# Input projection, retention, group norms and attention heads: from four programs a layer to two

## The reference, cut to what matters

```python
h = rmsnorm(x, norms[0]) * (1 + sc1) + sh1
aq, ak, av, af, bq, bk, bv, bg, ca, cb = split_cols(jnp.dot(h, w_in))
logf = jax.nn.log_sigmoid((af + b_f).astype(F32))
o_a = attn_fn(aq, ak, av, logf)                       # 4 heads x 128, causal softmax with a bias
q_b, k_b = rope(bq, pos), rope(bk, pos) * (DKB ** -0.5)
r, ret_s = retention(q_b, k_b, bv, ret_s0, ret_chunk) # 4 heads x 64, chunks of 128 tokens
r = _standardize(r).reshape(n, L, WB) * ret_gn_g
o_b = r * jax.nn.silu(bg)
u = ca * jax.nn.sigmoid(cb)
cv, conv_state = causal_dwconv(conv_ctx, u, conv_w, conv_b)   # 31 taps, 256 channels
o_c = jax.nn.silu(layernorm(cv, conv_ln_g, conv_ln_b))
mix = jnp.dot(jnp.concatenate([o_a, o_b, o_c], axis=-1), w_o)
x = x + g1 * rmsnorm(mix, norms[1])
```

## Time and profile before

| what | value |
|---|---|
| median of 3 runs | 3267.7 us (3264.27 to 3270.58) |
| the profiled execution, its own time | 3262.0 us |
| its span, from the first to the last instruction | 3260.2 us |
| PE busy | 2951.3 us (91% of the span) |
| DVE busy | 1751.8 us (54%) |
| ACT busy | 1146.1 us (35%) |
| POOL busy | 336.8 us (10%) |
| mean granted TensorE clock | 0.925 |

### The profile page before, as it was taken

The page is one execution under the profiler, slowest core; times in us unless marked ns, Lnnn a source line. Parts: engine busy times, 40 slices in busy tenths (PEclk is TensorE's granted clock), DMA queues, the critical chain, the costliest instruction groups (busy, mean ns, idle before and its releaser), DMA issues. The chain is left out here.

```text
span 3260.2 us, 45129 instructions
## 1 busy us (share of the span) xinstructions
PE 2951.3 (91%) x17756; PEld 2467.0 (76%) x17756; DVE 1751.8 (54%) x2765; ACT 1146.1 (35%) x1825; POOL 336.8 (10%) x166
## 2 busy tenths in 40 slices
PE   6798789979999999999767997998799999999996
PEld 3586477748878889999726865777388788899996
DVE  1396322243676676676615943223446766766765
ACT  1231123224444354444312311233235444454442
POOL 4111001013200000000042200100231000000000
PEclk7897699989999999999868966999799999999998
DMA  8311011143223332333182100111422333332331
GB/s 329 100 39 24 14 40 32 32 130 97 79 90 97 91 97 90 93 91 91 42 324 55 36 13 21 33 33 45 147 87 84 93 95 91 97 92 85 98 91 68
DMA packets 366283, 276.03 MB, mean 85 GB/s; under 512 B 24125, under 2 KB 308325, under 8 KB 365822
## 3 DMA queue, kind: packets, MB, share of 16 engines
q1 hardware_dynamic: 354896, 267.27, 26.3%
q10 hardware_dynamic: 11214, 6.41, 0.6%
HBM read 259.22 MB, written 15.26 MB: 84 GB/s over the span
## 5 line engine op out<-in xcount | busy, mean ns | idle before, releaser
L1536 PE MATMUL tslot<-g_hi,w_hi 128*128 128x260 f32 (+1 forms) x2496 | 672.9, 324 | 7.6 <-DVE g_lo L2065 6.1
L1536 PE MATMUL tslot<-g_hi,w_lo 128*128 128x260 f32 (+1 forms) x2496 | 667.0, 322 | 0.0
L1536 PE MATMUL tslot<-g_lo,w_hi 128*128 128x260 f32 (+1 forms) x2496 | 664.8, 321 | 0.0
L1536 PEld LDWEIGHTS tslot<-g_hi,w_hi 128*128 128x128 f32 x2496 | 416.4, 190 | 48.9 <-DVE g_lo L2065 6.2
L1536 PEld LDWEIGHTS tslot<-g_hi,w_lo 128*128 128x128 f32 x2496 | 415.4, 189 | 37.9
L1536 PEld LDWEIGHTS tslot<-g_lo,w_hi 128*128 128x128 f32 x2496 | 415.5, 190 | 37.4
L1507 ACT ACTIVATE w_hi<-w_raw 128x1024 fp32r<-128x1024 f32 x292 | 307.1, 1052 | 315.4 <-PE tslot L1854 311.8
L2126 DVE TENSOR_TENSOR cat<-cat,tslot 128x512 f32<-128x512 f32 (+1 forms) x320 | 220.4, 690 | 192.5 <-PE tslot L1854 191.3
L1511 DVE TENSOR_TENSOR w_lo<-w_raw,w_hi 128x1024 fp32r<-128x1024 f32 x256 | 311.8, 1218 | 0.0
L1854 PE MATMUL tslot<-f_hi,w_hi 128*128 128x260 f32 (+1 forms) x1056 | 283.6, 323 | 6.7 <-DVE w_lo L1511 4.5
L1854 PE MATMUL tslot<-f_hi,w_lo 128*128 128x260 f32 (+1 forms) x1056 | 282.0, 322 | 0.0
(11 more groups left out here) (320 smaller groups left out, 4052.8 us busy)
## 6 DMA issues: line engine op xcount, KB each, us to landing
w_raw<-in_ffn_up_dram SPq DMA_DIRECT2D x176, 512.0 KB, 3.7
a_raw<-in_ada_w_dram SPq DMA_DIRECT2D x24, 2048.0 KB, 17.1
w_raw<-in_ffn_down_dram SPq DMA_DIRECT2D x88, 512.0 KB, 3.3
w_raw<-in_w_in_dram SPq DMA_DIRECT2D x46, 512.0 KB, 3.9
w_raw<-in_w_o_dram SPq DMA_DIRECT2D x32, 512.0 KB, 3.7
kp<-in_cache_k_dram SPq DMA_DIRECT2D x32, 256.0 KB, 3.0
xrow<-in_x_prompt_dram SPq DMA_DIRECT2D x8, 512.0 KB, 8.8
out_k_prompt_dram<-k_tok SPq DMA_DIRECT2D x8, 512.0 KB
```

Source lines behind the costliest of these rows:

```text
L1536: last = pe.matmul(out[:, at + a:at + b], w[:, kk, :], x[:, kk, t0 + a:t0 + b], start=(kk == 0 and first), stop=(kk == KD - 1 and w is w_lo))
```

## The change

`block_retention`, `block_group_norms` and `block_heads` become one program, `block_mixer`, and the last two tiles of `block_project` (the gates, i = 10 and 11) move into it. A layer has one barrier where there were three. The mixer makes 14 tiles in 42 passes: each tile in three passes of 344 columns, one pass 24 matmuls. Behind each pass all engines do a fixed piece of other work: retention chunks in phases 1 to 9, group norms in phases 11 to 31, attention in phases 9 to 45, nine phases a head. The gates' tiles are the last two, passes 36 to 41.

Twelve of the 62 taps leave `block_project` and are done by VectorE in phases 1 to 12. The low parts of tiles 1 to 13 are made by VectorE (`low`) in the mixer; that of its first tile is made by GpSimd at the end of `block_project`.

The mixer needs room, so the residual `k.x` is written to a tensor in device memory (`x_hold`) during `block_project`, its place serves the mixer as working space, and it is read back in `block_samples`. The convolution's input `u` moves into `cat` 4 and 5 without its 30 zero columns; a tap now covers only the columns that it reaches.

The diff, cut to its core:

```diff
+TAPS_EARLY = 50
+def conv_tap(k, dve, n):
+    j, w = divmod(n, CONV_W)
+    w = CTX - w
+    u, acc = k.cat[:, 4 + j, :], k.cat[:, 6 + j, CTX - w:TP]
...
+    return dve.scalar_tensor_tensor(acc, u[:, 0:TP - CTX + w], k.vecs[:, 1, 2 * w + j:2 * w + j + 1], acc, ALU.mult, ALU.add)
 def block_project(k, L):
-    tiles = [COL_CA, COL_CA + DC, COL_CA + P, COL_CA + DC + P] + [COL_BQ + P * j for j in range(8)]
+    tiles = [COL_CA, COL_CA + DC, COL_CA + P, COL_CA + DC + P] + [COL_BQ + P * j for j in range(6)]
-        u = sb("u", [P, 2, CTX + NT])
+        u = k.cat[:, 4:6, :]
-            for m, col in enumerate([COL_F] + tiles):
+            for m, col in enumerate([COL_F] + tiles + [2 * HA * DA]):
...
             sp.dma_start(d["conv_sample"][L, :, 0:CTX - 1, :], d["state_conv"][L, :, 1:CTX, :]).then_inc(stored, 16)
+            sp.dma_start(k.x_hold.rearrange("p (a b) -> p a b", b=NT), k.x[:, :, :]).then_inc(stored, 16)
...
-                taps(at, at + 8)
-                at += 8
+                if i < 7:
+                    taps(at, at + 8)
+                    at += 8
...
-            taps(at, len(todo))
+PASS = ((0, 344), (344, 688), (688, NT))
+def block_mixer(k, L):
+        @block.sync
+            def load(n):
+                if n >= 3:
+                    sp.wait_ge(lo_done, n - 2)
+                sp.dma_start(k.w_raw[n % 2][:, :, :], w_in[:, :, column(n):column(n) + P]).then_inc(loaded[n % 2], 16)
...
+        @block.tensor
+            def dense_pass(p):
+                n, (a, b) = p // 3, PASS[p % 3]
+                if p % 3 == 0 and n >= 1:
+                    pe.wait_ge(lo_done, n)
+                if p >= 2:
+                    pe.wait_ge(evac, p - 1)
+                for kk in range(KD):
+                    for w, x, first in ((w_hi, k.h_hi, True), (w_hi, k.h_lo, False), (w_lo, k.h_hi, False)):
+                        last = pe.matmul(dense[p % 2][:, 0:b - a], w[:, kk, :], x[:, kk, a:b], ...)
+                last.then_inc(pass_done, 1)
...
+            for p in range(LAST):
+                if p < N_PASS:
+                    dense_pass(p)
+                h, at = phase(p)
+                if p == 0:
+                    samples()
+                if 2 <= p <= 9:
+                    back(p - 2)
+                if 1 <= p <= 8:
+                    front(p - 1)
+                if p >= 9:
+                    attention(h, at)
+                if 12 <= p < 21:
+                    norm_sums(p - 12)
+                if 11 <= p < 20:
+                    norm_mean(p - 11)
+                if 23 <= p < 32:
+                    norm_rows(p - 23)
+        @block.scalar
...
+                if n >= 3 * HA:
+                    act.activation(k.cat[:, 4 + n - 3 * HA, a:b], out, ACT.Silu).then_inc(evac, 1)
...
+        @block.vector
+            for p in range(LAST):
+                if p == 0:
+                    low(1)
+                    samples_out()
+                if 1 <= p <= 8:
+                    prepare(p - 1)
+                if 1 <= p <= 2 * CONV_W - TAPS_EARLY:
+                    clink(conv_tap(k, dve, TAPS_EARLY + p - 1))
+                if 2 <= p <= 9:
+                    update(p - 2)
...
+                if p % 3 == 2 and (p + 4) // 3 < N_TILES:
+                    low((p + 4) // 3)
 def block_samples(k, L):
             ahead.load(sp)
+            sp.dma_start(k.x[:, :, :], k.x_hold.rearrange("p (a b) -> p a b", b=NT)).then_inc(x_back, 16)
+            sp.wait_ge(x_back, 16)
 def trunk(nc, dram):
-                    run(block_retention, L)
-                    run(block_group_norms, L)
-                run(block_heads, L)
+                    run(block_mixer, L)
```

More of the change, by code:

```diff
@@ L732, in block_retention @@
-        vst = sb("vst", [P, 2 * S, DB])
         small = sb("small", [P, 2, 2 * S])
         pre = sb("pre", [P, NC8 * HA])
[L735 to L742, removed]
+        s0 = prob[0][:, :].rearrange("p (a s e) -> p a s e", a=2, s=S)
@@ L823, in _, with turn_blocks @@
-            pe.wait_ge(state_loaded, 32)
-            for hh in range(2):
-                for s in range(S):
-                    for hp in range(2):
-                        rows = slice(64 * hp, 64 * hp + 64)
-                        last = pe.matmul(o_bank[rows, S * hh + s:S * hh + s + 1], s0[rows, hh, s, :],
-                                         qr[rows, hh, TP + s:TP + s + 1], start=True, stop=True)
-            last.then_inc(samp_ready, 1)
-            for c in range(NC8):
-                if c + 1 < NC8:
-                    front(c + 1)
-                back(c)
+            def turn_blocks(src):
+                for c in range(NC8):
+                    last = pe.transpose(turn[:, P * c:P * c + P], src[:, P * c:P * c + P], ident)
+                last.then_inc(turned, 1)
@@ new lines, in spread_bias, with turn_values @@
+            def spread_bias(h):
+                pe.wait_ge(diag_ready, h + 1)
+                if h == 0:
+                    pe.wait_ge(att_done, NC8)
+                else:
+                    pe.wait_ge(top, NC8 * h)
+                for a, b in HALVES:
+                    last = pe.matmul(sc[:, a:b], ones, bias[:, a:b], start=True, stop=True)
+                last.then_inc(bias_ready, 1)
+            def turn_values(h):
+                if h == 0:
+                    pe.wait_ge(kv_moved, NC8)
+                else:
+                    pe.wait_ge(p_moved, NC8 * h)
+                pe.wait_ge(evac, 9 * h + 3)
+                turn_blocks(vf)
@@ new lines, in turn_keys @@
+            def turn_keys(h):
+                pe.wait_ge(tok_moved, 3 * h + 1)
+                pe.wait_ge(evac, 9 * h + 9)
+                turn_blocks(kf[h % 2])
+                if h == 0:
+                    pe.wait_ge(r_moved, NC8)
+                else:
+                    pe.wait_ge(o_moved, NC8 * h)
+                for n, src in enumerate((kf[h % 2], vf)):
+                    last = pe.matmul(o_bank[0:S, P * n:P * n + P], src[:, TP:NT], ident, start=True, stop=True)
+                last.then_inc(turned, 1)
@@ new lines, in values @@
+            def values(h, i):
+                pe.wait_ge(p_moved, NC8 * h + i + 1)
+                if i < 4:
+                    pe.wait_ge(tok_moved, 3 * h + 3)
+                    if i == 2:
+                        pe.wait_ge(o_moved, NC8 * h + 2)
+                else:
+                    pe.wait_ge(o_moved, NC8 * h + i)
+                at = P * (i % 4)
+                for c in range(i + 1):
+                    row = P * (ROW_AT[i] + c)
+                    last = pe.matmul(o_bank[:, at:at + P], v_tok[h % 2][:, P * c:P * c + P], prob_t[:, row:row + P],
+                                     start=(c == 0), stop=(c == i))
+                last.then_inc(o_ready, 1)
```

893 lines of the change are left out of this document (465 added, 428 removed).

## The result

The changed kernel took 3097.1 us (median of 4 runs, 3092.6 to 3099.0), the kernel before on the same chip 3266.0 (3262.7 to 3270.6). The ratio is 0.948, with a 95% interval of 0.9463 to 0.9496: 169 us less, where 133 less had been forecast. The profiled execution has a span of 3096.3 us against 3260.2.

The account below looks back on a forecast made before the run. TensorE was taken as the bound, losing time to idle waits, three barriers and a low clock. Terms summed to 353.0 us a layer against 419.7, 133.4 less over two layers, giving 3134; own range 3100 to 3160, 8 in 10 reaching 3205.

Parts of the forecast that it names:

- barrier in front, barrier behind: Either side of the merged program: 2.8 us for last read-out and barrier, 1.6 us for the barrier to the samples' program.
- Retention: Retention chunks: 4.2 us each at the full clock, 33.6 us for eight; bounds 3.9 and 7.77 a chunk.
- Rival A: Retention phases: the clock falls again because chunks are too thin to hold it; 3221, or 3178 for half; chance 0.2.
- Heads: Attention with each head's own three tiles: 61.6 us of TensorE busy time a head, 246.4 a layer, idle 7.4 a head gone.
- New passes: At the 42 dense passes: weight loads can't run ahead over a wait, 0.24 us each, 10.1 us a layer.
- Norms: Group norms: means 7.6, spread 9.5 and sums of squares 8.0, together 25.1 us against a stretch of 41.7.
- Projection: Projection without gate tiles: ends with ScalarE's read-out of tile i = 9, begun at 268.46; VectorE ends near 267.1.
- Taps, low parts, table loads, residual: Side work on VectorE, ScalarE and transfers: hidden under passes or other work, so nothing added to the sum.
- B: Attention phases: fixed engine order lets late steps stop those behind, 54 us a layer; 3242, half 3188; chance 0.12.
- C: Last tiles, phases 36 to 41: ScalarE's table loads are on the path, 15.4 us a layer; 3165; chance 0.05.
- D: The residual's write and read-back: its transfers stand out, 12 us a layer; 3158; chance 0.04.
- E: First 32 phases: small pieces keep the clock at 0.50, 253 us more a layer, about 3640, slower; chance 0.04.

Follow-up runs that it names:

- both improvements: Changed kernel with tile 10's high part made before ScalarE's swap copies in the projection, and 16 taps moved to the mixer in place of 12: 3084.7 us, ratio 0.9456.

## Why the prediction came out as it did

The mechanism was right: a full clock in the retention, and passes that cover the waits. The forecast was 37 us too high, nearly all of it in one group of terms: the merged stretch is 17.5 us shorter than forecast in the first layer and 19.1 in the second (353.0 less 335.5 and 333.9). Some smaller things cancel by luck: between the two profiled executions the time fell by 163.8 us, 6.7 less than the two stretches gave (84.2 + 86.3), while the 5.7 us that the forecast added from profiled execution to median were not there in the changed kernel (3098.2 and 3097.1). Per layer, from the end of tile i = 9, with the starts of the phases on TensorE's timeline (a pass's 24 products 3.88 us apart from start to next; phase 0 11.08, phase 1 5.06, phases 2 to 8 8.48 each):

| term | forecast | measured |
|---|---|---|
| barrier in front, barrier behind | 2.8 + 1.6 | 2.65 + 1.6 |
| phases 0 to 8 and `back(7)`: samples' part, 8 chunks, 9 passes, clock at the start | 5.7 + 33.6 + 34.0 + 2.2 + 2.0 = 77.5 | 11.08 + 5.06 + 7 x 8.48 + 3.3 = 78.8 |
| the other 33 passes | 33 x 3.78 = 124.7 | 33 x 3.88 = 128.0 |
| attention, norms, gaps at 33 passes, uncovered end | 110.4 + 25.1 + 7.9 + 3.0 = 146.4 | 335.5 less the rest = 124.5 |
| sum | 353.0 | 335.5 |

**Retention.** Right, with its size a little off: a chunk costs 8.48 - 3.88 = 4.6 us, not 4.2; 0.4 x 8 = 3.2 us a layer. The upper end of the bound, 7.77, was real: cutting the passes gave it back, and a wait. The lower end, 3.9, was not reached: at a clock of 1.00 a pair of products takes 0.72 us where it took 1.22 at 0.50, so not all of a chunk follows the clock. Rival A asked whether a chunk can hold the clock once it is begun. It can, behind a pass; alone it can't.

**The term that was mis-sized** is "attention, norms and the pieces behind the passes", 146.4 us for 124.5. 4.0 of the measured ones are idle time (2.9 + 1.1, forecast 3.0), so the work itself took 120.5. Phases 32 to 40 hold the nine attention pieces of one head and no norms, each behind a pass, and let the rest be divided:

```profile
517.62:576.43 58.81, 58.81 (x382) 53.49 (x381) 20.33 (x56) 33.05 (x49) 0.00 (x0) 1.00 0.06 19
```

Less nine passes of 3.88 this is 23.9 us of attention a head, where the forecast had 27.6 (61.6 less nine passes). The stretch from phase 9 to 31, 174.5 us, less its 23 passes, `back(7)` and the attention in it leaves some 22 us for the norms. So the 21.9 us too many divide, in the order of their size:

- "Heads", 61.6 us busy each: 3.7 us a head too much, 15 in all. Busy time up to a wait holds the modelled end of the last product before it. The head of the earlier trace rows, 480 to 549, had nine waits of TensorE, six of them for ScalarE's copy; in the changed kernel there is none in the middle. The same four instructions, before the change and after it:

```profile
529.78 1.51 PE L1153 MATMUL hslot<-kf,q 128*128 128x512 f32 x4
```

```profile
575.27 1.51 PE L962 MATMUL sc<-x_res 128*128 128x512 f32 x4
```

Before, the wait of 2.19 us is counted from their end, 1.51 us after their start; after, the next pass starts at 576.43, 1.16 after it. Nine times some 0.35 us is most of the 3.7; that all nine are alike is an estimate.
- "New passes", 42 x 0.24 = 10.1, of which 7.9 are in this term. TensorE has no gap at a pass: its idle time in the merged program is 5.66 us, and that at the end. The 0.24 was taken from weight loads that stood behind a wait; with the semaphore long given most of it is gone. What is left stands in the rows of the passes: 3.88 us in place of 3.78, since the second product of a pass starts 0.26 us behind the first and not 0.16. That is 0.1 each, 4.2 us a layer for 10.1.
- "Norms", 25.1, added from the busy times of groups, some 3 too many. Such a sum counts the time in which instructions overlap twice. The changed kernel shows it: its groups for norms add up to 24.8 us, as forecast, for some 22 of time, and those for attention to 119.8, for four times 23.9. The forecast knew that ends are modelled and gave 4 us a layer for it in the heads, as a lower end.

Against these stand some 4 us at the end that had no term: 1.0 of idle time more than forecast, and about 3 of work without a pass, half of it the 14 instructions at the low clock (3.26 us in place of 1.72).

**Projection.** Right within 4 us: the tile ends 3.4 us earlier (265.0, 1 us of it from an earlier start of the projection) and so does VectorE (263.3, forecast 267.1). Before the change the eight taps took 12.54 us, with one low part of GpSimd beside them; put back with none beside them they took 10.35.

**Taps, low parts, table loads, residual.** All four were costed at nothing, with the cover named; all four were tested and held: the taps' price without the move is 30.6 us (forecast "some 16 us" a layer), the low parts' is nothing on either engine, the table loads' nothing, the read-back has some 6 us of room. The samples' program is 52.9 us, 1.6 more than 51.3; that small loss had no term. 1.1 of it lies in one row of 32 products (16.71 us in place of 15.65) whose clock comes up later; TensorE waits for the read-back nowhere.

**Rivals.** A, B, C and D each have a run that speaks against them; E is out by the clock of 1.00 from 278.8 on. B was nearest at ScalarE's Silu of the convolution, by 1.9 us. The dip that E feared exists only in phase 0 (11.15 us at 0.72), for which 2.0 us had been set, and for three microseconds behind the last pass.

## What to carry to other kernels

An engine that is busy all the time may still run at half its clock: here a retention with no idle TensorE took 7.77 us a chunk, and a chunk with 24 wide products in front took 8.33. Look for the clock in the stretch first, then ask what dense work lies elsewhere in the layer and can be put between the thin pieces; the same passes also hide the waits of 2.1 and 2.6 us that the thin pieces have for other engines. When you add a sum from such a profile, take the distance from start to start on the timeline and not the busy times of groups, and a gap that stood behind a wait loses most of its price once the wait is gone (0.1 us of 0.24 here). After a merge, look at what ends the stage that was shortened: twice here the next engine in line (ScalarE's order, then VectorE's taps) held a few more us.

## What the runs showed of the hardware

- The chunks of the retention did not bring the clock up by themselves: 61.4 us at 0.50 before, with TensorE hardly ever idle, and 0.50 again in the run with passes 1 to 8 cut. One pass of 24 products of 344 columns ahead of each chunk gives 1.00 throughout, in two different kernels. The Trainium skill, *TensorE: Matmul & The Clock Gate*, "Part 4: PE-mode transpose", says that transposes do not count as busy for the clock in the same way; of a chunk's 20 products only four are transposes, and no run here tells them from the other small products. So the agreement that the prediction saw in the 0.50 is weak.
- An elementwise step of VectorE in fp32 can slow down while GpSimd makes a low part. With both improvements on, the rotary step L704 of the projection takes 3.43 us beside it, and 1.23 with GpSimd idle:

```profile
251.39 3.39 POOL L579 TENSOR_TENSOR w_lo<-w_raw,w_hi 128x1024 fp32r<-128x1024 f32 x1 [3.81 <-ACT w_hi L627]
252.44 3.43 DVE L704 TENSOR_TENSOR swap<-swap,rope 128x1032 f32<-128x1032 f32 x1
```

Eight taps took 14.36 us with two low parts beside them and 10.35 without, and the low part 3.39 in place of 2.37. In the merged program VectorE loses 3.9 us to it over thirteen low parts, and the time shows nothing of that, since VectorE is idle for more than half of it. In the projection, which VectorE ends, low parts made by VectorE (1.22 us each) might be worth more than the 2 us that such a collision costs; this wasn't tried.
- The issue of the 4.2 MB read-back keeps SP for 3.15 us behind the other loads, where two loads of 512 KB took 2.37 together. It is not a price of its size: in the run with two read-backs the first took 3.26 us to issue and the second, made when the first had landed, 0.34; and they landed after 16.0 and 12.3 us.
